# Gate/up weights of an expert in two transfers of 2 MB in place of four of 1 MB

## The reference

```python
    def expert_block(args):
        x_blk, e = args
        a = x_blk @ w_gate[e]
        u = x_blk @ w_up[e]
        return (jax.nn.silu(a) * u) @ w_down[e]

    yb = lax.map(expert_block, (xb, block_e)).reshape(cap, d)
    return jnp.zeros((n_tok, d), h.dtype).at[buf_tok].add(buf_w[:, None] * yb)
```

## Time and profile before

| | |
|---|---|
| median of three runs | 1769.44 us (1765.87 to 1773.49) |
| profiled execution, its own time | 1765.99 us |
| its span, first to last instruction | 1764.4 us |
| PE busy | 1744.0 us, 99% of the span |
| granted TensorE clock, mean | 0.998 |
| gate/up transfers on SP's queue | 128 of 1024 KB |
| down transfers on SP's queue | 64 of 1024 KB |

### The profile page before, as it was taken

The page is one execution under the profiler, slowest core; times in us unless marked ns, Lnnn a source line. Parts: engine busy times, 40 slices in busy tenths (PEclk is TensorE's granted clock), DMA queues, the critical chain, the costliest instruction groups (busy, mean ns, idle before and its releaser), DMA issues. The chain is left out here.

```text
span 1764.4 us, 27701 instructions
## 1 busy us (share of the span) xinstructions
PE 1744.0 (99%) x10013; PEld 1394.3 (79%) x10013; DVE 933.6 (53%) x1913; ACT 236.3 (13%) x618; POOL 679.4 (39%) x755
## 2 busy tenths in 40 slices
PE   9999999999999999999999999999999999999997
PEld 8888758888578887588895678877777778887776
DVE  5556785378773677763785792433423233223332
ACT  2021110211101211102210201011111001101011
POOL 5933312045221235130341124445455455554552
PEclk9999999999999999999999999999999999999999
DMA  7663752444733437423444489998999999998984
GB/s 293 224 215 116 295 167 85 127 148 165 253 112 104 144 114 270 154 96 126 153 136 140 164 337 339 342 343 325 343 350 330 344 353 340 344 339 332 349 325 179
DMA packets 135755, 415.31 MB, mean 235 GB/s; under 512 B 54838, under 2 KB 69486, under 8 KB 102320
## 3 DMA queue, kind: packets, MB, share of 16 engines
q1 hardware_dynamic: 57488, 316.78, 48.5%
q0 software_dynamic: 26880, 58.91, 9.4%
q10 hardware_dynamic: 51248, 37.82, 6.6%
HBM read 370.78 MB, written 68.72 MB: 249 GB/s over the span
## 5 line engine op out<-in xcount | busy, mean ns | idle before, releaser
L1132 PE MATMUL ps_proj<-hnT,wo 128*128 128x128 f32 (+4 forms) x992 | 199.5, 283 | 0.0
L1134 PE MATMUL ps_proj<-hnT,wo 128*128 128x128 f32 (+4 forms) x992 | 197.7, 281 | 0.0
L1132 PEld LDWEIGHTS ps_proj<-hnT,wo 128*128 128x128 f32 x992 | 153.8, 191 | 13.6 <-issue 13.6
L1742 POOL DMA_INDIRECT xin<-hn_rows,idx_quad x116 | 117.3, 1011 | 122.2 <-DVE hnT L2733 46.5
L1134 PEld LDWEIGHTS ps_proj<-hnT,wo 128*128 128x128 f32 x992 | 153.1, 191 | 0.0
L744 PE MATMUL ps_proj<-hnT,ww 128*128 128x256 f32 x640 | 151.9, 379 | 0.0
L744 PEld LDWEIGHTS ps_proj<-hnT,ww 128*128 128x128 f32 x640 | 119.8, 190 | 16.6 <-issue 1.4
L1581 POOL TENSOR_TENSOR xres<-ww 128x512 f32<-128x512 f32 x12 | 15.2, 1267 | 289.1 <-DMA ww<-in_w_slots 255.1
L2964 DVE SCALAR_TENSOR_TENSOR hn<-xin,rsy,ww 128x1024 f32<-128x1024 f32 x30 | 38.5, 1285 | 133.5 <-POOL rsy L1800 133.5
L1132 PE MATMUL ps_rows<-hnT,wo 128*128 128x128 f32 (+4 forms) x496 | 98.9, 281 | 0.0
L1132 PE MATMUL ps_scores<-hnT,wo 128*128 128x128 f32 (+4 forms) x496 | 98.8, 281 | 0.0
(11 more groups left out here) (522 smaller groups left out, 3487.2 us busy)
## 6 DMA issues: line engine op xcount, KB each, us to landing
wo<-in_w_gu SPq DMA_DIRECT2D x128, 1024.0 KB, 7.5
ww<-in_w_slots SPq DMA_DIRECT2D x43, 1024.0 KB, 5.0
og<-in_w_dn SPq DMA_DIRECT2D x32, 1024.0 KB
vx<-in_w_dn SPq DMA_DIRECT2D x32, 1024.0 KB
xin<-in_x SPq DMA_DIRECT2D x16, 512.0 KB, 5.5
ww<-w_v_sums SPq DMA_DIRECT2D x16, 512.0 KB, 4.3
xres<-in_x SPq DMA_DIRECT2D x16, 512.0 KB, 5.4
x_rows<-x ACTq DMA_DIRECT2D x16, 512.0 KB, 3.3
```

Of the source, the lines that this page charges most:

```text
L1132: pe.matmul(GU[m][:, 0:n_], wo[:, kt, m * P:(m + 1) * P], xT[:, kt, 0:n_], start=(kt == 0), stop=(kt == KT - 1), skip_group_check=True)
L1134: mm = pe.matmul(GU[m][:, CAP:CAP + n_], wo[:, kt, FF + m * P:FF + (m + 1) * P], xT[:, kt, 0:n_], start=False, stop=(kt == KT - 1), skip_g ...
L1742: pool.indirect_dma_start(xg[:, t * TC:(t + 1) * TC], None, hn2_d.rearrange("s (j c) -> (s j) c", j=TQ), bass.IndirectOffsetOnAxis(ap=idx_ ...
```

## The change

The gate/up weights of an expert are packed in two halves of 2 MB. `NWS` is 2, and `PER`, the number of steps that one transfer holds, is 4. SP issues two transfers per expert, PE counts `wgu_used` up after step 3 and at the end, and waits before steps 0 and 4. Of the first expert, the first half is issued where the first piece was, and the second half where the other three pieces were. The second piece of its down weights (into vx) waits for the last store of the normalised rows (`hn2_stored1`) in place of the gather of the first tail (`x4_gathered`).

```diff
-        NWS = KT // 2
-        wgu = [wo[:, 2 * j:2 * j + 2, :].rearrange("p a n -> p (a n)") for j in range(NWS)]
+        NWS = 2
+        PER = KT // NWS
+        wgu = [wo[:, PER * j:PER * (j + 1), :].rearrange("p a n -> p (a n)") for j in range(NWS)]
...
                 sp.wait_ge(S_("out_part_done"), out_part_end(NB - 1, 1, 7))
-                gate_up_piece(0, 0)
+                for j in range(NWS // 2):
+                    gate_up_piece(0, j)
                 sp.wait_ge(S_("out_part_done"), out_part_end(NB - 1, 1, 4))
                 sp.wait_ge(S_("x_gathered"), 16)
-                for j in range(1, NWS):
+                for j in range(NWS // 2, NWS):
                     gate_up_piece(0, j)
-                sp.wait_ge(S_("x4_gathered"), 16)
+                sp.wait_ge(S_("hn2_stored1"), 16 * NTILE // 2)
                 down_piece(0, 1)
...
-                    if kt % 2 == 0:
-                        pe.wait_ge(S_(f"wgu_loaded{kt // 2}"), 16)
+                    if kt % PER == 0:
+                        pe.wait_ge(S_(f"wgu_loaded{kt // PER}"), 16)
...
-                pe.wait_ge(S_(f"wgu_loaded{NWS - 1}"), 16)
...
-                    if kt % 2 == 1:
+                    if kt % PER == PER - 1:
                         mm.then_inc(S_("wgu_used"), 1)
...
-                    if kt % 2 == 0 and m == 0:
-                        pe.wait_ge(S_(f"wgu_loaded{kt // 2}"), (k + 1) * 16)
+                    if kt % PER == 0 and m == 0:
+                        pe.wait_ge(S_(f"wgu_loaded{kt // PER}"), (k + 1) * 16)
...
-                    if kt < KT - 2 and m == FT - 1 and kt % 2 == 1:
+                    if kt < KT - 2 and m == FT - 1 and kt % PER == PER - 1:
                         mm.then_inc(S_("wgu_used"), 1)
```

More of the change, by code:

```diff
@@ L3050, in _packed @@
     gate, up = [w.reshape(ne, P, d // P, ff).transpose(0, 2, 1, 3) for w in (gate, up)]
-    both = np.stack([gate.reshape(ne, d // 256, 2, P, ff), up.reshape(ne, d // 256, 2, P, ff)], axis=4)
+    both = np.stack([gate.reshape(ne, 2, d // 256, P, ff), up.reshape(ne, 2, d // 256, P, ff)], axis=4)
     rows = [i["norm_mix"][0]] + [b_in[c:c + dm] for c in (0, dm, conv, conv + dm, conv + 2 * dm)] + list(conv_w)
@@ L3059, in _packed @@
         "late": np.concatenate([i["norm_ffn"][0], i["b_group"][0], i["b_expert"][0]]), "norm_final": i["norm_final"],
-        "w_gu": both.transpose(0, 1, 3, 2, 4, 5).reshape(ne, d // 256, P, 4 * ff),
+        "w_gu": both.transpose(0, 1, 3, 2, 4, 5).reshape(ne, 2, P, d // P * ff),
         "w_dn": down.reshape(ne, ff // 256, 2, P, d).transpose(0, 1, 3, 2, 4).reshape(ne, ff // 256, P, 2 * d),
```

## The result

The changed kernel took 1778.34 us in the median, 1.0045 of the kernel before, with a 95% interval of 1.003 to 1.0061; a second set of runs of the same kernel (below) gave 1.0024 (1.0013 to 1.0035). The median is that of seven executions, one of which took 2023.75 us at a granted clock of 0.849; the ratio leaves that one out. The change makes the kernel slower, by 4 to 8 us. The forecast was no change, at 1768.7 us. The profiled execution took 1776.61 us against 1765.99, 10.6 us more.

A forecast was written before the change was run, and what follows sets the result against it. PE was taken as the bound, busy 1744.0 of 1764.4 us. From the profiled 1765.99 us, -0.7 (second gather) and 0 (loop) gave 1765.3 us, or 1768.7 against the median of 1769.44; range 1761 to 1783 us.

The forecast's parts named there:

- the tail's gather in the first expert: First expert: with the vx piece as company the gather lands up to 2.8 us later, just absorbed before PE's need at 1021.61.
- The second gather: Second expert's gather of rows has less beside it: PE's 1.4 us wait shrinks, bounds 0 and 1.4, taken as -0.7 us.
- Later release, fewer waits and issues: Expert loop: 2 MB land in 9.5 us against 14.0 available; dropped PE waits, counts and SP issues gain nothing: 0 us.
- the rival of the late halves: Expert loop: a half takes 15.7 us against 14.0, PE waits 1.7 us in 30 experts, +51 us, 1820 us; chance 0.04.
- Rows of 16 KB: Expert loop: longer rows delay residual gathers by 1.9 us (bounds 0 and 2.8), scatters by 0.3; absorbed by the chain, 0 us.
- One of the tightest places: Expert loop: DVE's hidden rows have 2.92 us of idle time before them, so leftover lateness counts only after that.
- The rival of the residual chain: Expert loop: gather and scatter grow beyond the 2.5 us absorbed per expert, lateness piles up, +21 us, 1790 us; chance 0.12.
- The test given for it: PE waiting at L1154, the down products, for hidden rows or banks would show the residual chain as the bound.
- The range: Whole kernel: 1761 to 1783 us, its upper end taking in an excess of the residual chain of some 0.55 us per expert.

The follow-up runs named there:

- e2: Kernel before, its four 1 MB transfers kept, with only the first expert's vx piece made to wait for the last store of normalised rows: 1774.7 us, 1.003.
- e1: Changed kernel with the first expert's vx piece, and the final norm's rows behind it, waiting again for the first tail's gather: 1771.53 us, 1.0011.
- e6: Changed kernel with the second expert's hidden rows moved ahead of the last block of the routing on DVE: 1771.6 us, 1.0012.
- e9: Changed kernel with the second expert's hidden rows and the turn of the third expert's tail both ahead of DVE's last routing block: 1771.16 us, 1.0006.
- e7: Changed kernel with the second expert's hidden rows earlier on DVE and two 8 KB rows per partition in each 2 MB transfer: 1770.4 us, 1.001.
- e5: Changed kernel with the vx piece behind the tail's gather again and DVE's overflow rows in two parts: 1771.59 us, 1.0011.
- e3: Changed kernel with each 2 MB transfer bringing two rows of 8 KB to a partition in place of one of 16 KB: 1.0025.
- e8: Changed kernel with each 2 MB transfer bringing four rows of 4 KB to a partition in place of one of 16 KB: 1.0025.
- e10: Kernel before, in 1 MB transfers, with the vx piece early and the second expert's hidden rows and the turn behind them earlier on DVE: 1769.42 us, 0.9998.

## Why the prediction was wrong

**The step that failed** is that of the tail's gather in the first expert: the up to 2.8 us by which it might be later, "so that the 2.8 is just absorbed". The size was a little low: the gather had landed within 2.8 us of its issue (1015.26 to 1018.06), and now DVE can begin only 6.4 us after it, some 3.5 us more. The step followed the turned rows to PE's late products at 1021.61, where 2.9 us were free, and there PE indeed lost only the 0.6 us that were over. The mistake is that it stopped there. It did not ask what stands behind the turn on DVE. That is the whole rest of the routing in order, without idle time, and at its end the second expert's hidden rows, for which PE was waiting 0.65 us already in the kernel before. That wait was a sign that the list had no slack, but the prediction looked only at waits above 1 us and, in the loop, from 1060 us on. A delay in a list with no slack arrives whole at its end: `e2` makes it alone, `e1` takes it away, `e6` and `e9` let it come and take away what it meets.

**What it cost** was then doubled by the clock, which the prediction did not consider. In all six profiles with a wait of 3.5 or 3.6 us there, a stretch at half clock follows, worth 3.0 us in the changed kernel and 1.7 to 3.0 in the six; behind the 2.0 and 2.1 us of `e6` and `e7` none follows. But the length of the wait does not decide it. In the mixer equal waits of PE at one line were followed by half clock in `e1` and not in `e9` (eight products in 5.37 and in 3.67 us):

```profile
214.27 5.37 PE L775 MATMUL ps_proj<-kT,uu 128*128 128x512 f32 x8 [2.16 <-issue]
...
211.06 3.67 PE L775 MATMUL ps_proj<-kT,uu 128*128 128x512 f32 x8 [2.13 <-issue]
```

So a wait is priced by more than its length. The Trainium skill (TensorE: Matmul & The Clock Gate, Part 1: The HAM clock gate) says that the clock is set by how busy PE has been recently; the trace agrees in that each of these stretches stands at or behind a wait of PE, such as the 3.58 us above.

**The second gather**: -0.7 us was forecast from bounds of 0 and -1.4. The upper bound was right: the wait is gone in every kernel with the early vx piece, and back at 1.2 and 1.6 us in `e1` and `e5`.

**Later release, fewer waits and issues**: right. 2 MB land in 9.3 us (forecast 9.5), PE waits for no half, and the rival of the late halves did not occur.

**Rows of 16 KB**: the term was +1.9 us per residual gather (bounds 0 and 2.8), absorbed by the chain. PE paid for a late gather only at the eleventh expert. But the average growth is not what the profiles show. These are DVE's waits from 1100 us on, of the changed kernel and of its second profile:

```profile
DVE xin L2929 <- DMA xin<-x_rows,idx: 78.3, 17, 8.3
DVE xin L2929 <- PE ps_num L1155: 42.6, 17, 2.7
...
DVE xin L2929 <- DMA xin<-x_rows,idx: 38.3, 16, 7.3
DVE xin L2929 <- PE ps_num L1155: 51.7, 23, 2.7
```

Before, the gathers came late 21 times and early 15 times, for 61.5 and 33.6 us, and in the second profile 24 and 13 times, for 68.9 and 28.5 us. The forecast was more of the first sum and less of the second. The first sum came out on either side of 61.5 us, the second rose, and fewer gathers were late with the change, not more. The one profile of the 16 KB rows whose view gives the landing of these gathers (`e5`, L1772) has this line:

```profile
DMA to landing us min/median/max: 4.2/6.8/12.0
```

Its median is 6.8 us, where 9.7 was forecast and 7.8 had been measured before; only the maximum is up, from 10.8 us. So the growth of 1.9 us for each gather was mis-sized: it did not occur in the median. What grew is the longest wait, from 5.3 and 4.9 us to 8.3 and 7.3. Nor is the length of the row alone the cause: with 2 MB in 8 KB rows the longest waits are 8.4 and 8.8 us, as with 16 KB (7.3 to 10.0), while with 1 MB in the same 8 KB rows they are 4.9 to 5.7 in four profiles. Only with 4 KB rows is it 4.4. By the rule of the Trainium skill that was cited (DMA: Bandwidth & Descriptors, queues, rings and completion order), turns are taken a packet at a time. With a row for a packet, as the counts of packets suggest (48272 with rows of 16 KB, 56464 in `e3`, 72848 in `e8`: one and three more for each of the 8192 rows), 8 KB rows would be back at the longest waits of before; they are not, and 4 KB rows are. What of this is the bunching of transfers by the later release and what is the row stays open.

**"One of the tightest places"**, with 2.92 us of idle time, was not one: two hidden rows stood directly behind DVE's own work, at 1053.07 and 1262.00 us, and it is there that PE waited. The rival of the residual chain is thus half right at the eleventh expert: a late gather reached PE there, for 1.95 us in the first profile and 0.4 in the second, through one long block of DVE and not as lateness that piles up over 30 experts. The test given for it, a wait at the down products, could not tell it from the delay in DVE's list. With the block split the two profiles have no wait there, and the time shows nothing measurable.

**The range**: 1778.34 us lies inside the 1761 to 1783 us that were stated, but by luck. The upper end was drawn for the residual chain, which did not cause the loss.

**Left open**: kernels with 2 MB and without the long wait lie at 1.0006 to 1.0012, the one with 1 MB at 0.9998. The intervals overlap, and the difference of 1.4 to 2.5 us is not accounted for: `e5` is the clearest case, with much the same waits as the kernel before and 1.0011 (1.0001 to 1.0021).

## What to carry to other kernels

When a transfer is moved beside another, follow the one it delays through the whole in-order list of the engine that waits for it, down to the next place where another engine waits for that list; slack found at the first consumer says nothing of the last. Look for instructions with no idle time ahead of them on an engine that seems half idle (DVE is busy 53% of the span here): it is they, not the average, that pass a delay on. And take two profiles of each kernel before a wait is called its own.

## What the runs showed of the hardware

The granted clock fell to its lower level for stretches of some 3.5 to 7 us at or behind single waits of PE, in the middle of a program at 0.994 to 0.998 on average. It is not certain to fall: near 109 us PE waits 3.0 to 4.2 us in every profile of these kernels, and a stretch follows in 12 of 14. It follows in the second profile of the kernel before (3.3 us of waiting, then sixteen products in 6.58 us), but not in the first (3.6 us, then the same products in 3.69). Shorter waits were followed by one as well: of 1.9 us once at 1006 us (second profile of the kernel before), and of 2.1 to 2.2 us between 211 and 215 us in `e1`, `e2` and `e8`, but not in `e9` and `e10`. Such a stretch costs 1.5 to 3 us in these rows. That is a good part of the spread of the runs before (1765.87 to 1773.49 us); that it makes the spread is not shown.
